# One recurrent stage split in two (projections streamed, then one scan over four groups), and the first two stages joined

## What is computed

```python
mod = (silu(c) @ w_ada + b_ada)
h = rmsnorm(x, norm1_g) * (1 + sc1) + sh1
(z, xs, bm, cm, dtr, q, k, v, qi, ki, wi, gs, ga) = split(h @ w_in)
xbc, new_conv = causal_conv(concat([xs, bm, cm]), conv_state, conv_w, conv_b)   # 4 taps, then silu
# per group g of 4 (8 heads x 64) and chunk c of 8 (128 tokens):
#   m = (C B^T) * exp(segment sums of dt*A), y = m (dt x) + exp(Acs) C state + d_skip x
#   state = state * chunk_decay + B^T (decay_end dt x)
y = y * silu(z); y = y * rsqrt(mean(y*y over the 512 of a group) + eps) * norm_g
```

## Time and profile before

| | us |
|---|---|
| median of three executions | 3235.45 |
| lowest, highest | 3233.89, 3241.91 |
| the profiled execution | 3245.16 |
| span of its instructions | 3243.4 |
| granted TensorE clock, mean over the span | 0.935 of 2.4 GHz |
| first two stages, to the first matmul of `project` | 0 to 81.7 |
| `ssm`, first matmul to its last store | 1105.8 to 1971.3 |

### The profile page before, as it was taken

The page is one execution under the profiler, slowest core; times in us unless marked ns, Lnnn a source line. Parts: engine busy times, 40 slices in busy tenths (PEclk is TensorE's granted clock), DMA queues, the critical chain, the costliest instruction groups (busy, mean ns, idle before and its releaser), DMA issues. The chain is left out here.

```text
span 3243.4 us, 39578 instructions
## 1 busy us (share of the span) xinstructions
PE 2934.5 (90%) x15831; PEld 2380.4 (73%) x15831; DVE 1595.4 (49%) x2860; ACT 729.8 (23%) x1511; POOL 715.6 (22%) x430
## 2 busy tenths in 40 slices
PE   6999999989986679999999974999879999999997
PEld 3888566657874556676775854999869898898986
DVE  1313499625541456536546464254563544445355
ACT  4121211126761114424324242000030000000001
POOL 0000520023200122222122232323232232232320
PEclk7999999989995779999999977999989999999999
DMA  6110245410012230121120105233211111111111
GB/s 194 37 66 20 66 137 162 129 49 2 2 39 73 94 86 23 47 78 39 48 75 29 40 26 186 78 112 98 88 31 60 39 39 53 39 46 46 40 40 53
DMA packets 220308, 211.59 MB, mean 65 GB/s; under 512 B 15257, under 2 KB 201489, under 8 KB 219938
## 3 DMA queue, kind: packets, MB, share of 16 engines
q1 hardware_dynamic: 195580, 162.36, 16.5%
q10 hardware_dynamic: 20944, 34.86, 3.1%
q0 software_dynamic: 3600, 11.82, 0.9%
HBM read 165.32 MB, written 43.83 MB: 64 GB/s over the span
## 5 line engine op out<-in xcount | busy, mean ns | idle before, releaser
L2052 PE MATMUL ps<-h_lo,w_hi 128*128 128x344 f32 x1504 | 483.0, 321 | 40.3 <-DVE h_lo L2160 33.5
L2054 PE MATMUL ps<-h_hi,w_lo 128*128 128x344 f32 x1504 | 481.5, 320 | 0.0
L2053 PE MATMUL ps<-h_hi,w_hi 128*128 128x344 f32 x1504 | 481.5, 320 | 0.0
L2052 PEld LDWEIGHTS ps<-h_lo,w_hi 128*128 128x128 f32 x1504 | 284.2, 189 | 42.0 <-issue 35.4
L2053 PEld LDWEIGHTS ps<-h_hi,w_hi 128*128 128x128 f32 x1504 | 283.9, 189 | 0.2
L2054 PEld LDWEIGHTS ps<-h_hi,w_lo 128*128 128x128 f32 x1504 | 284.0, 189 | 0.0
L2034 POOL CAST w_hi<-w_raw 128x2048 fp32r<-128x2048 f32 (+1 forms) x50 | 97.3, 1945 | 838.1 <-PE ps L2054 803.4
L1514 PE MATMUL ps<-hT,ring 128*128 128x344 f32 x864 | 266.7, 465 | 0.0
L1593 PE MATMUL ps<-ring,hT 128*128 128x256 f32 x1024 | 236.3, 393 | 7.8 <-PEq L1164 6.7
L453 PE MATMUL ps<-ring,hT 128*128 128x256 f32 (+3 forms) x1152 | 238.1, 369 | 1.0 <-PEq L214 1.0
L1514 PEld LDWEIGHTS ps<-hT,ring 128*128 128x128 f32 x864 | 168.2, 197 | 92.6 <-issue 19.1
(11 more groups left out here) (393 smaller groups left out, 5025.5 us busy)
## 6 DMA issues: line engine op xcount, KB each, us to landing
ring<-in_w_ada SPq DMA_DIRECT2D x24, 1024.0 KB, 7.5
ring<-in_w_in SPq DMA_DIRECT2D x23, 1024.0 KB, 5.2
w_raw<-in_w_ffn_in SPq DMA_DIRECT2D x44, 512.0 KB, 5.2
ring<-in_w_in SPq DMA_DIRECT2D x24, 512.0 KB, 8.3
w_raw<-in_w_ffn_out SPq DMA_DIRECT2D x10, 1024.0 KB, 5.0
s_sig<-sig ACTq DMA_DIRECT2D x16, 516.0 KB, 6.9
x<-s_sig ACTq DMA_DIRECT2D x16, 516.0 KB, 3.4
stt<-in_state_ssm SPq DMA_DIRECT2D x32, 256.0 KB, 3.9
```

Source lines behind the costliest of these rows:

```text
L2052: nc.tensor.matmul(out, ah, bl, start=(i == 0), stop=False)
L2053: nc.tensor.matmul(out, ah, bh, start=False, stop=False)
L2054: mm = nc.tensor.matmul(out, al, bh, start=False, stop=(i == len(terms) - 1))
```

## The change

`modulation` and `norm_stage` become one stage, `first_norm`. POOL issues all nine tiles of x at the start, into nine buffers. PE does the transposes of tiles before the products of each piece of `w_ada` (`turns_before`), the turned tiles go to `hT` unmodulated (DVE moves the lower four blocks, ACT the upper four), and when `modT` is ready DVE and ACT apply it to `hT` in place, four instructions of 128x1024 each.

`ssm` becomes `stream` and `scan`. `stream` runs 102 units of 8 matmuls with 344 columns, z units too (features on partitions; the last columns of a z block are the samples'), through four banks of PSUM. ACT stores each convolved block to `s_post` (24 of 512 KB) and each block of z to `s_z` (16 of 512 KB). The convolutions and the sample steps of the groups stand beside the units at written positions (`raw_at`, `spread_at`, `sum_at`). `scan` takes 32 steps, n = 4 c + g, so that groups alternate; each step loads its 6 blocks of `s_post` and 4 of `s_z` (four buffers deep), and most of what was single is doubled, PSUM banks apart. The gate, the norm and norm_g are applied after y is turned: the squares are summed over partitions by two matmuls with ones, the root is taken of 128x128, and the reciprocal of 128x128.

```diff
+def first_norm(K, hT, source):
...
+        turns_before = [2, 2, 2, 2, 1, 0, 0, 0]
...
+            for t in range(9):
+                pool.dma_start(x[0:rows_of(t), t, :], source(t)).then_inc(x_in[t], 16)
...
+            def move_high(t):
+                act.wait_ge(turned, 2 * t + 2)
+                nc.scalar.copy(hT[:, 4:8, P * t:P * t + P],
+                               ps[:, TURNS + 2 * (t % 2) + 1, :].rearrange("p (k n) -> p k n", k=4)).then_inc(high_moved, 1)
...
+            square(0)
+            for t in range(TT):
+                square(t + 1)
+                move_high(t)
+            act.wait_ge(modT_step, 3)
+            act.wait_ge(low_moved, TT)
+            act.wait_ge(high_moved, TT)
+            for k in range(4, KB):
+                nc.scalar.activation(hT[:, k, 0:SEQ], hT[:, k, 0:SEQ], ACT.Identity, bias=K.modT[:, 0, k, 0:1],
+                                     scale=K.modT[:, 1, k, 0:1])
+
...
+            for i in range(n_slabs):
+                for _ in range(turns_before[i]):
+                    if t + 1 < 9:
+                        divide(t + 1)
+                    if t < TT:
+                        move_low(t)
+                    t += 1
+                add_bias(i)
...
+            dve.wait_ge(low_moved, TT)
+            for k in range(4):
+                v.tensor_scalar(hT[:, k, 0:SEQ], hT[:, k, 0:SEQ], K.modT[:, 1, k, 0:1], K.modT[:, 0, k, 0:1],
+                                ALU.mult, ALU.add)
...
+            for i in range(n_slabs):
+                for _ in range(turns_before[i]):
+                    turn(t)
...
+def stream(K, hT, S):
...
+        blocks = [("z", 0, j) for j in range(4)]
+        for g in range(1, GROUPS):
+            blocks += [("x", g, f) for f in range(FBS)] + [("z", g, j) for j in range(4)]
+        NU = TC * len(blocks)
+        z_end = [12 + 30 * g for g in range(GROUPS)]
+        raw_at = [11 if g == 0 else z_end[g] - 10 for g in range(GROUPS)]
+        spread_at = [[raw_at[g] + 3, raw_at[g] + 7] for g in range(GROUPS)]
+        sum_at = [raw_at[g] + 12 for g in range(GROUPS)]
...
+            def unit(u):
+                i, c = u // TC, u % TC
+                n = first + i // 2
+                if u % (2 * TC) == 0:
+                    pe.wait_ge(*ring_landed(K, n))
+                if u >= 4:
+                    kind, before = blocks[(u - 4) // TC][0], (u - 4) // TC
+                    pe.wait_ge(*((z_done if kind == "z" else pre_done), TC * nth(kind, before) + (u - 4) % TC + 1))
+                w = slab_of(K, n)
                 for k in range(KB):
+                    a = mm(ps[:, u % 4, 0:CW], w[:, k, P * (i % 2):P * (i % 2) + P], hT[:, k, CW * c:CW * c + CW],
+                           start=(k == 0), stop=(k == KB - 1))
...
+            def silu(q):
+                act.wait_ge(conv_done, q + 1)
+                a.activation(post[:, q % NPOST, :], post[:, q % NPOST, :], ACT.Silu).then_inc(post_done, 1)
+                act.wait_ge(post_done, q + 1)
+                act.dma_start(A["s_post"][q], post[:, q % NPOST, :]).then_inc(post_out[q % NPOST], 16)
...
+            sample_conv(0)
+            sample_states(0, 0)
+            convolve(1, 0)
+            sample_states(0, 1)
+            convolve(1, 1)
+            sample_gate(0)
+            convolve(1, 2)
+            sample_norm(0)
+            for f in range(3, FBS):
+                convolve(1, f)
+            for g in range(1, GROUPS):
+                sample_conv(g)
+                sample_states(g, 0)
+                sample_states(g, 1)
+                sample_gate(g)
+                sample_norm(g)
+                if g + 1 < GROUPS:
+                    for f in range(FBS):
+                        convolve(g + 1, f)
+
...
+def scan(K, S):
+    nc, A, ps = K.nc, K.A, K.ps
+    N = TT * GROUPS
+    NIN, NOUT = 4, 3
...
+                sp.dma_start(post[:, n % NIN], A["s_post"].rearrange("f p n -> p f n")[:, FBS * g:FBS * g + FBS, cols])\
+                    .then_inc(post_in[n % NIN], 16)
+                if n >= NIN:
+                    sp.wait_ge(ygated, n - NIN + 1)
+                sp.dma_start(z[:, n % NIN], A["s_z"].rearrange("f p n -> p f n")[:, 4 * g:4 * g + 4, cols])\
+                    .then_inc(z_in[n % NIN], 16)
...
+            for n in range(N + 3):
+                if n < N:
+                    weigh(n)
+                if n + 2 < N:
+                    segments(n + 2)
+                if 2 <= n < N + 2:
+                    fold(n - 2)
+                if n >= 3:
+                    store(n - 3)
...
+            def turn(n):
+                c = at(n)[0]
+                pe.wait_ge(*((y_ready, n - GROUPS + 1) if c else (yd_done, n + 1)))
+                if n:
+                    pe.wait_ge(yroot, n)
+                for j in range(4):
+                    t = tr(ps[:, TURNED, P * j:P * j + P], y[:, n % 2, P * j:P * j + P], K.ident[:])
+                t.then_inc(yT_ps, 1)
+
+            def sum_squares(n):
+                pe.wait_ge(yfolded, n + 1)
+                for j in range(2):
+                    t = mm(ps[:, TURNED, 0:P], K.ones[:], ysq[:, n % 2, P * j:P * j + P], start=(j == 0), stop=(j == 1))
+                t.then_inc(ysum_ps, 1)
+
...
+            front(0)
+            for n in range(N + 2):
+                if n + 1 < N:
+                    front(n + 1)
+                if n < N:
+                    diagonal(n)
+                if n >= 2:
+                    sum_squares(n - 2)
+                if n < N:
+                    recur(n)
+                if 1 <= n <= N:
+                    turn(n - 1)
+            for g in range(GROUPS):
+                final_state(N - GROUPS + g)
...
+            def decay(n):
+                act.wait_ge(xt_ps, n + 1)
+                if n >= 2:
+                    act.wait_ge(xw_done, n - 1)
+                    act.wait_ge(xd_done, n - 1)
+                a.copy(xt[:, n % 2], ps[:, XT, :]).then_inc(xt_done, 1)
+                act.wait_ge(seg_ps, n + 1)
+                if n >= 2:
+                    act.wait_ge(yd_ps, n - 1)
+                a.activation(m[:, n % 2].rearrange("p h l -> p (h l)"), ps[:, SEG:SEG + 2, :].rearrange("p a n -> p (a n)"),
+                             ACT.Exp).then_inc(m_exp, 1)
+
+            def root(n):
+                act.wait_ge(ysum_ps, n + 1)
+                if n >= 2:
+                    act.wait_ge(ynormed, n - 1)
+                a.activation(spreads[:, n % 2, :], ps[:, TURNED, 0:P], ACT.Sqrt, bias=eps[:, 0:1], scale=1.0 / GW).then_inc(yroot, 1)
+
+            def square(n):
+                act.wait_ge(ygated, n + 1)
+                if n >= 2:
+                    act.wait_ge(ysum_ps, n - 1)
+                a.activation(ysq[:, n % 2], yT[:, n % NOUT].rearrange("p k n -> p (k n)"), ACT.Square).then_inc(ysquared, 1)
+
+            def out(n):
+                g = at(n)[1]
+                act.wait_ge(ynormed, n + 1)
+                for j in range(4):
+                    k = 136 + 4 * g + j
+                    o = a.activation(yT[:, n % NOUT, j, :], yT[:, n % NOUT, j, :], ACT.Copy, scale=K.vecs[:, k:k + 1])
+                o.then_inc(yT_done, 1)
...
+            decay(0)
+            for n in range(N + 2):
+                if n + 1 < N:
+                    decay(n + 1)
+                if n >= 2:
+                    root(n - 2)
+                if 1 <= n <= N:
+                    square(n - 1)
+                if n >= 2:
+                    out(n - 2)
...
+            def combine(n):
+                c, g = at(n)
+                yc = y[:, n % 2]
+                dve.wait_ge(yd_ps, n + 1)
+                dve.wait_ge(xd_done, n + 1)
+                if n >= 2:
+                    dve.wait_ge(yT_ps, n - 1)
+                v.tensor_tensor(yc, ps[:, DIAG_Y, :], xd[:, n % 2], ALU.add).then_inc(yd_done, 1)
+                if c:
+                    t = yoff[:, n % 2]
+                    dve.wait_ge(yo_ps, n - GROUPS + 1)
+                    if n >= GROUPS + 2:
+                        dve.wait_ge(y_ready, n - GROUPS - 1)
+                    v.tensor_tensor(by_head(t), by_head(ps[:, OFF_Y, :]), head_cols(S.e_acs, n), ALU.mult).then_inc(yo_done, 1)
+                    dve.wait_ge(yo_done, n - GROUPS + 1)
+                    dve.wait_ge(yd_done, n + 1)
+                    v.tensor_tensor(yc, yc, t, ALU.add).then_inc(y_ready, 1)
+                    dve.wait_ge(s_done, n - GROUPS + 1)
+                    sh = by_head(state[:, g])
+                    v.tensor_tensor(sh, sh, head_cols(S.c_dec, n), ALU.mult).then_inc(s_scaled, 1)
+                    dve.wait_ge(s_scaled, n - GROUPS + 1)
...
+            def gate(n):
+                dve.wait_ge(yT_ps, n + 1)
+                dve.wait_ge(z_in[n % NIN], 16 * (n // NIN + 1))
+                if n >= NOUT:
+                    dve.wait_ge(yT_out[n % NOUT], 16 * (n // NOUT))
+                v.tensor_tensor(yT[:, n % NOUT], ps[:, TURNED, :].rearrange("p (k n) -> p k n", k=4), z[:, n % NIN],
```

(69 more changed lines are left out.)

914 lines of the change are left out of this document (374 added, 540 removed).

## The result

The changed kernel took 3281.36 us in the median of four runs (3276.37 to 3282.17), the kernel before 3235.81 beside it: a ratio of 1.0125, with a 95% interval of 1.0109 to 1.0141. That is 45.6 us slower; 3228 was predicted, with 3194 to 3256 as the range. The profiled execution of after took 3276.37 us, 31.2 more than the profiled one of before (3245.2). I account for those 31.2 us, since the rows belong to them.

What follows compares the result with a forecast made beforehand. PE, 90% busy, bounds the kernel; in the new scan a ring through DVE and ACT. Joined first stages -25.5, recurrent stage +18.5 (507 + 377 = 884 against 865.5): -7 us, 3228 on the median, range 3194 to 3256.

Steps and rivals of the forecast that it cites:

- Nor is POOL: Scan step: POOL is not in the ring, being busy 4.6 us per chunk, plus a fold of 256 columns.
- the ring: Scan step: once round DVE, then ACT's scalings, copy, table load and exponential, back to m; 11.6 us a step.
- POOL's segments stand beside m, as in the row of 1.96: Scan step: m runs beside POOL's segments as in an earlier profile row, where it took 1.96 us.
- the bound of 2.79: Scan step: m took between 1.21 and 2.79 us over all chunks, bounding a step by 10.9 and 12.4.
- the table's drain: ACT's table switches in the scan: a rule's further 1.38 us each, making a step 13.0; the prediction left it out.
- The join: First stages joined: project starts at 56 instead of 81.7 us, 25.5 less; bounds 15 and 30 less.
- The stream: Recurrent stage's projections: 472 us of units plus work between, slow start and end, 507 us, PE without waits.
- PE sets the step: Rival, scan: at the lower clock throughout, PE's step is 14.8 us; 81 us more, 3309; 8%.
- The switch costs double: Rival, scan: a second 1.3 us for the table switch in the ring; 34 us more, 3262; 5%.
- Samples hold PE up: Rival, stream: sample steps still hold PE up, 18 us in each group; 70 us more, 3298; 5%.
- No ring: Rival, scan: exponential ready in time, DVE alone sets the step at 8.4 us; 83 us less, 3145; 7%.
- a step whose m waits for anything but ACT makes the ring wrong: Sign for the profile after, in scan: DVE should idle some 3 us a step before m, waiting for ACT.

Runs made afterwards that it cites:

- e3: The changed kernel with the root replaced by an exponential of the same 128 columns, so no table load between; ratio 1.0119 to the kernel before, step 13.27 us.
- e8: The changed kernel with m taking its second factor from PSUM (C B without the mask); ratio 0.9946 to the kernel before, step 11.23 us.
- e2: The changed kernel with GpSimd's segments(n+2) also waiting for VectorE's state scaling, so not beside m; ratio 0.9974 to the kernel before, step 11.42 us.
- e5: e2 without GpSimd's fold, TensorE summing four blocks of squares instead of two; ratio 0.9938 to the kernel before, step 10.99 us.
- e10: e9 with the loads of x from its third tile on waiting for the first piece of w_ada; ratio 0.9644 to the kernel before.
- e4: The changed kernel with four more matmuls of 256 columns a step on TensorE, output unchanged; ratio 1.0149 to the kernel before, step 13.27 us.
- e9: e7 with GpSimd's xw, segments, xd and store placed beside VectorE instructions that read PSUM; ratio 0.9635 to the kernel before, step 7.64 us.
- e6: The changed kernel with ScalarE's copy and exponential of step n+2 right behind the root of n-2; ratio 0.9894 to the kernel before, step 10.80 us.
- e7: The changed kernel with the edits of e5 and e6 together; ratio 0.9720 to the kernel before, step 8.53 us.
- e12: The changed kernel with fold(n - 2) called ahead of segments(n + 2) on GpSimd, no added wait; ratio 0.9980 to the kernel before, step 11.51 us.

## Why the prediction was wrong

The step that failed is "Nor is POOL" in the ring, which went by POOL's busy time (4.6 us a step), and with it "POOL's segments stand beside m, as in the row of 1.96" and the bound of 2.79. The part of the mechanism that held is a ring through DVE's step and ACT's scalings, with PE and the table's drain not in it. Its other half was wrong: in after it does not come back through ACT's copy, load and exponential (e3) but through POOL. From the end of the scalings (1785.88) the store, xw, xd and segments take until 1790.88, 5.0 us, and m ends 1.09 later. By ACT's links m would have ended at 1789.92 (1788.71 + 1.21), 2.05 earlier. Where m can't be held, in e8, the predicted ring is there at close to its size: 11.23, against the 10.9 given for the shortest m and 0.43 for the held division.

I took 1.96 as the price of m beside the segments. It was a start time in disguise: in the earlier trace rows the segments had begun 1.02 us ahead of m, so only 0.9 of them were left to wait for. In the new list they begin 0.27 us after m, and m is held for 2.17. The row held both the ends from which this could be read; I never placed GpSimd's instructions, its store among them, in the new step.

Term by term, forecast and measured:

| term | forecast | measured |
|---|---|---|
| `project` starts (joined stages) | 56 (-25.5) | 62.4 (-19.3) |
| stream | 507 | 501.9 |
| scan, first load to m of step 5 | 47 | 45.0 |
| a step: m to reciprocal | 5.9 | 7.02 |
| reciprocal | 1.0 | 0.98 |
| division | 0.7 | 1.16 |
| scalings | 1.15 | 1.18 |
| copy, load, exponential | 2.9 | 2.93 |
| step | 11.65 | 13.27 |
| 26 steps | 302 | 343.1 |
| last m to last issue | 28 | 31.3 |

- **The step.** The excess of 1.6 us is m (3.25 for 1.96, 0.17 of it given back by the instructions behind it) and the division (1.16 for 0.7 to the scalings' start), both held by GpSimd; 26 of them are 41 us. The terms of the table add up to 44 too many; less the 5.2 us that came off ahead of and behind the stage, this is the 38 by which the profiled execution missed 3238. e2, e5 and e8 each remove one of them and win it. The new reciprocal, where I saw the doubt, was 0.94, as taken.
- **The join.** Forecast too high by 6.2 us. The first products began at 15.5 instead of 12, since two tiles took 3.73 (two later ones, at a granted clock of 1.00, 2.2) and the first piece landed 2.1 later still; the pieces then cost 2.2 more than taken, 1.7 of it the first, which took 5.27 where the later ones took 3.62; the passes at the end cost 0.7. The first piece shows why it was slow: its first eight products started 0.43 us apart, the next eight, from 18.86 on, 0.21, and the trace's clock record begins at 18.85 with 1.00. That the two slow tiles are the same cause is likely, but the record has no clock so early. PE's slow start, priced for the stream and the scan, was left out of this sum. x and pieces share the transfers, and e10 shows that serving one first only moves the wait.
- **The stream.** 497.1 of 501.9 us busy, clock 0.99; the one gap in PE above 0.05 us is 3.14, under the last group's samples, which were forecast to stick out. The other sample steps are hidden. The 5 us less than forecast are the three sums of squares between units (0.9 us each instead of 1.9) and the end (6.1 instead of 8). That these and the 5.2 us elsewhere came off is luck: none was forecast, and without them the miss would be 10 us larger.
- **The rivals.** PE sets the step: excluded by e4. The switch costs double: excluded by the rows around the load, which leave no room for a drain; the time of e3 couldn't tell, since the load is not in the ring. Samples hold PE up: not seen. "No ring": what e9 made it, at 7.64 us a step where that rival had 8.4. The case that came was on no list: a ring that closes through POOL. The range is said to leave out 14%; by the chances listed PE and the samples are 13, and with the two halves 19.
- **The rule "a step whose m waits for anything but ACT makes the ring wrong".** The profile says that m waited for ACT's exponential (1.64 us idle), and yet e3 shows that the exponential could come 1.3 us sooner for nothing. The true last wait, for POOL, was inside m's own duration, and by this rule the ring was wrong.

The medians differ by 45.6, the profiled executions by 31.2: that of before lay 9 us above the median of its runs, that of after 5 below. I have no cause for either beyond the spread of the runs.

## What to carry to other kernels

An instruction that waits for a port shows no idle time: it shows a long duration. When one VectorE instruction with both inputs in SBUF has several durations (here 1.21, 1.96, 2.79), compare its end with the end of the GpSimd instruction beside it before taking any of them as a price, and place GpSimd's instructions, the transfers that it issues included, in the new order as carefully as the bound engine's. Put them beside VectorE instructions that read PSUM, and test a chain by taking a link out of it: if nothing moves, another chain at least as long stands beside it.

## What the runs showed of the hardware

- A VectorE instruction with both inputs in SBUF ended 1.08 to 1.09 us (1024 elements) or 0.55 to 0.56 (512) after the GpSimd instruction that held it, in the kernel before, in after, e2, e3, e6 and e7. With one input in PSUM it took its own 1.22.
- Between two GpSimd instructions the waiting one sometimes gets in and sometimes not. In after, m was recorded 0.27 us ahead of the segments and still came after them; in e3 it was passed over twice, in e6 the sum likewise. In the third step of after m was recorded 0.23 us ahead of the segments and got in (1.35 us), and the segments took 2.88. In e12 the division got in, and the segments were held (2.34 for 1.90). The Trainium skill (SBUF — State Buffer, Who interferes with whom) lets the one that issues first have the ports; m in after had been waiting longer and did not get them. What decides it, no run here settles.
- GpSimd's xw began 0.02 us after the recorded end (0.79 us long) of the store ahead of it in its list, in every step of the steady scan of after, and in e6 too, where the copy that it needs had been done for 6.8 us or more.
- The granted clock in the scan was 0.83 of 2.4 GHz on the mean, between its levels of 1.2 and 2.4, with PE busy for 69% of the window (after), and 0.99 with PE busy for 96% (e9).
